# One pool of four PSUM banks for scores and transposes in three attentions, and the sink column written behind each score

## The chip, the cores and the metric

The kernel runs on 1 core of one Trainium2 chip. The metric is device time in microseconds (us) of one execution. TensorE is called PE below, VectorE DVE, ScalarE ACT, GpSimd POOL, SyncE SP. PSUM, the memory that PE writes its results to, has eight banks here, b0 to b7, each 128 partitions by 512 float32.

## The reference

Three transformer blocks in a row on 512 tokens of width 1024, all in float32:

```python
def reference(x, ...):
    x = first_block(x, ...)    # pooling mixer + attention of 8 heads, gates, then an MLP
    return second_block(x, ...)

def second_block(x, p, ...):
    h = x
    for i in range(2):
        hn = rms_norm(h, attn_norm[i])
        if i % 2 == 0:
            mix = diff_attention(hn, ...)   # 8 heads, softmax(q1 k1) - lambda * softmax(q2 k2), over all 512 keys
        else:
            mix = windowed_gqa(hn, ...)     # 16 query heads, 4 kv heads, |i-j| <= 128, a sink logit per head
        h = h + mix
        h = h + conv_ffn(rms_norm(h, ffn_norm[i]), ...)
        gate = sigmoid(rms_norm(h, ple_norm[i]) @ ple_w_gate[i])
        h = h + (p[i] @ ple_w_proj[i]) * gate
    return rms_norm(h, final_norm)
```

In the sliding attention the sink enters the softmax as one more column: `m = max(max(s), sink)`, `pr = exp(s - m) / (sum(exp(s - m)) + exp(sink - m))`. With sequence 512 the first attention is causal with a slope per head (both key blocks of 256 are attended to where they lie in the past).

## The kernel before, in words

Every matrix product is done in three passes of float32r on split operands (high times high, high times low, low times high). So each step of a linear layer is three matmuls of 128x512 (lines 393, 394, 395), and splitting the weights is work for ACT (line 283) and POOL (line 239).

Python builds one table of steps, and each engine's program runs through that table from top to bottom and issues what is its own. Every engine works in the order of the table and blocks at the first wait that is not yet met. The table's order comes from a small planner at build time. `Schedule` keeps a clock for PE, DVE, ACT and POOL, and `duration` gives each step a planned length. `Flow.run` holds a list of waiting processes, each with a function that returns the events it needs. A step on DVE, ACT or POOL is placed when its events are planned to be ready at PE's clock plus `AHEAD` (0.4 us). A PE step of an attention (scores, transposes, products with V) is placed when its events are `MARGIN` (0.2 us) old on PE's clock. Where none is ripe, the next step of the linear layers is placed. So the linear layers of later heads, and the output projection where it can begin, fill PE between the steps of an attention.

An attention works in blocks of 128 queries, four per head. The chain of one block is:

- `scores`: the score matmuls (lines 407, 408, 409), kind "score". They contract over 64 rows, so two of them run side by side, one on rows 0 to 63 and one on rows 64 to 127 of the array: two heads in `attention_pairs`, the two softmaxes of one head in `attention_diff`. Such a pair takes two banks, b2 and b3 (`sbk`), and `need` asks that both are free.
- `soft`: in the first and third attention DVE adds the mask and takes the row minimum of the negated score in one custom instruction (kind "mask_min", line 599, followed by a short read of its accumulator). That frees the score bank. ACT then takes the exponential (line 328), DVE the reciprocal (line 578), and DVE (line 603) or POOL (line 264) normalizes. In the second attention DVE takes row maxima (line 574), ACT two exponentials (line 323, which free the banks), DVE reciprocal, ratio and the combination of the two (line 586).
- `turns_of`: PE transposes the block (line 415, kind "turn"), into b4 and b5 in turn (`tbk`). ACT (line 334) and DVE (line 621, "turn_low") bring it to SBUF as high and low parts, and the DVE step frees the bank. `v_tile` uses the same two banks for the transposes of V.
- `products_of`: the products with V (lines 438 and 439, in the second attention 426 to 428) into b6 (`obk`).

Linear layers use b0 and b1 (`LB2`) while an attention runs; b7 is for norms.

In the third attention the sink logit must stand in column 384 of the score bank when mask_min reads it; the score itself fills columns up to 384. Head t always has the same bank (b2 for even t, b3 for odd), so `sinks` writes the column once per head: for heads 0 and 1 ahead of all scores, for head t + 2 directly behind the last mask_min of head t (kind "sink_column", line 608, a DVE copy of 128x1). That makes 16 copies.

## Time and profile before

| what | value |
|---|---|
| median of 3 runs | 1973.62 us (1973.46 to 1975.21) |
| profiled execution: first to last instruction | 1972.9 us |
| PE busy | 1940.0 us, 98% |
| DVE busy | 1188.4 us, 60% |
| ACT busy | 924.4 us, 47% |
| POOL busy | 1109.2 us, 56% |
| granted PE clock, mean | 0.997 |

The times of the runs and the span of the profiled execution lie within 0.1% of each other. A PE busy share counts a matmul from its start to a modelled end, and the next one starts before that end, so a stretch can be "busy" although its matmuls start further apart than they could. Start-to-start times of the timeline tell more than the share. The three attentions lie at about 40 to 130 us, 732 to 950 us and 1407 to 1540 us of the span.

### The profile page before, as it was taken

What the parts mean: (1) busy time and instruction counts of PE and PEld (TensorE: products, weight loads), DVE (VectorE), ACT (ScalarE), POOL (GpSimd) and SP (SyncE); (2) the same over time, 40 slices, a digit from 0 to 9 for tenths busy, and PEclk for the clock granted to TensorE, in tenths of its full rate; (3) what the DMA queues carried; (4) which work ended last, traced back from release to release, by engine and by line L of the source; (5) the groups of instructions that cost most, each with busy time, mean ns of one, the idle gap of its engine ahead of it and who ended that gap; (6) DMA issues with size and microseconds to landing.
All of it is one profiled execution on the core that took longest, in us unless ns stands there. A gap on an engine that the chain in (4) does not pass through costs nothing.

```text
span 1972.9 us, 25163 instructions
## 1 busy us (share of the span) xinstructions
PE 1940.0 (98%) x9232; PEld 1590.0 (81%) x9232; DVE 1188.4 (60%) x1952; ACT 924.4 (47%) x1740; POOL 1109.2 (56%) x842
## 2 busy tenths in 40 slices
PE   8999999999999999999999999999999999999997
PEld 6877888888888877777888888888777888888886
DVE  6773325353433488877675646856688675746855
ACT  5653336533333366555453433445477543443443
POOL 5345544454444456454576665755785576666662
PEclk9999999999999999999999999999999999999998
DMA  4122233232232321111322222223110323222321
GB/s 160 65 70 96 89 114 128 95 104 102 97 111 94 111 98 68 45 65 54 128 103 100 97 96 97 97 90 109 65 54 33 128 97 107 97 86 96 107 93 57
DMA packets 52106, 182.72 MB, mean 93 GB/s; under 512 B 5776, under 2 KB 6160, under 8 KB 51984
## 3 DMA queue, kind: packets, MB, share of 16 engines
q1 hardware_dynamic: 51984, 181.12, 26.4%
q8 instruction: 74, 1.21, 0.2%
q14 instruction: 48, 0.39, 0.1%
HBM read 174.80 MB, written 6.29 MB: 92 GB/s over the span
## 4 chain that ended last, share of the span: by engine, by line
PE 92%; DVE 5%; ACT 1%; issue 1%; DMA 0%; POOL 0%; SPq 0%; DVEq 0%; ACTq 0%; POOLq 0%
PE b L393 28%; PE b L395 28%; PE b L394 28%; PE b L415 2%; PE b L407 1%; PE b L448 1%; PE b L439 1%; PE b L438 1%; DVE sm L574 1%; PE b L408 1%; PE b L409 1%; DVE ra L621 1%; DVE fa L586 0%; PE b L426 0%; DVE ra L483 0%
## 5 line engine op out<-in xcount | busy, mean ns | idle before, releaser
L239 POOL TENSOR_TENSOR ra<-raw,ra 128x512 fp32r<-128x512 f32 x632 | 883.2, 1405 | 771.7 <-ACT ra L283 770.0
L393 PE MATMUL b<-ra 128*128 128x512 f32 x2528 | 1000.7, 396 | 15.9 <-POOL ra L239 9.4
L395 PE MATMUL b<-ra 128*128 128x512 f32 x2528 | 985.9, 390 | 0.0
L394 PE MATMUL b<-ra 128*128 128x512 f32 x2528 | 985.2, 390 | 0.0
L283 ACT ACTIVATE ra<-raw 128x512 fp32r<-128x512 f32 x632 | 392.8, 628 | 531.9 <-PE b L395 526.4
L393 PEld LDWEIGHTS b<-ra 128*128 128x128 f32 x2528 | 475.5, 188 | 121.2 <-issue 15.2
L395 PEld LDWEIGHTS b<-ra 128*128 128x128 f32 x2528 | 475.0, 188 | 101.0
L394 PEld LDWEIGHTS b<-ra 128*128 128x128 f32 x2528 | 475.7, 188 | 93.3
L737 DVE TENSOR_TENSOR h<-b,h 128x512 f32<-128x512 f32 x136 | 91.8, 683 | 61.4 <-PE b L395 60.6
L628 DVE TENSOR_TENSOR tmp<-b,rb 128x512 f32<-128x512 f32 x62 | 42.4, 689 | 100.2 <-PE b L395 100.0
L621 DVE TENSOR_TENSOR ra<-b,ra 128x512 fp32r<-128x512 f32 (+4 forms) x166 | 91.9, 567 | 17.6 <-ACT ra L334 14.8
L628 DVE TENSOR_TENSOR gbuf<-b,rb 128x512 f32<-128x512 f32 x54 | 37.1, 690 | 107.7 <-PE b L395 107.5
L334 ACT ACTIVATE ra<-b 128x512 fp32r<-128x512 f32 (+3 forms) x142 | 67.9, 485 | 70.7 <-PE b L415 69.2
L707 DVE TENSOR_TENSOR fa<-b,fa 128x512 f32<-128x512 f32 x56 | 38.6, 689 | 78.8 <-PE b L395 78.8
L291 ACT ACTIVATE ra<-tmp 128x512 fp32r<-128x512 f32 x79 | 49.0, 626 | 56.4 <-DVE tmp L756 19.2
L415 PE MATMUL b<-ident,fa 128*128 128x128 f32 x368 | 63.2, 281 | 3.0 <-DVE ra L621 1.6
L328 ACT ACTIVATE fa<-fa,sm 128x257 f32<-128x257 f32 (+5 forms) x96 | 53.4, 558 | 23.3 <-DVE sm L599 23.0
L483 DVE TENSOR_TENSOR ra<-tmp,ra 128x512 fp32r<-128x512 f32 x60 | 59.4, 1007 | 2.9 <-ACT ra L291 2.4
L415 PEld LDWEIGHTS b<-ident,fa 128*128 128x128 f32 x368 | 41.0, 140 | 21.3 <-issue 9.2
L291 ACT ACTIVATE ra<-gbuf 128x512 fp32r<-128x512 f32 x58 | 36.0, 627 | 43.5 <-DVE gbuf L756 19.9
L489 DVE SCALAR_TENSOR_TENSOR ra<-h,vec,ra 128x512 fp32r<-128x512 f32 x40 | 44.8, 1124 | 9.1 <-ACT ra L296 9.1
L574 DVE TENSOR_REDUCE sm<-b 128x1 f32<-128x512 f32 x64 | 41.0, 681 | 14.9 <-PE b L409 14.7
(276 smaller groups left out, 1900.4 us busy)
## 6 DMA issues: line engine op xcount, KB each, us to landing
raw<-in_f_g SPq DMA_DIRECT2D x40, 512.0 KB, 3.5
raw<-in_f_v SPq DMA_DIRECT2D x40, 512.0 KB, 3.5
raw<-in_f_d SPq DMA_DIRECT2D x40, 512.0 KB, 3.5
raw<-in_w_up SPq DMA_DIRECT2D x32, 512.0 KB, 3.5
raw<-in_w_down SPq DMA_DIRECT2D x32, 512.0 KB, 3.5
raw<-in_p_g SPq DMA_DIRECT2D x16, 512.0 KB, 3.5
raw<-in_w_gp SPq DMA_DIRECT2D x8, 512.0 KB, 3.4
raw<-in_w_ga SPq DMA_DIRECT2D x8, 512.0 KB, 3.4
```

The lines of the kernel that those rows point to most:

```text
L239: e.tensor_tensor(wl, src, wh.bitcast(F), ALU.subtract).then_inc(*w_low.mark(n))
L283: e.activation(wh, src, ACT.Copy).then_inc(*w_high.mark(n))
L291: e.activation(dst, src, ACT.Copy).then_inc(*high.mark(n))
L334: e.activation(dst, src, ACT.Copy).then_inc(*high.mark(n))
L393: e.matmul(ps, wh[:, c:c + 128], xh, start=start, stop=False)
L394: e.matmul(ps, wh[:, c:c + 128], xl, start=False, stop=False)
L395: last = e.matmul(ps, wl[:, c:c + 128], xh, start=False, stop=stop)
L415: x = e.transpose(m.banks[b][:, 128 * q:128 * q + 128], src[:, 128 * q:128 * q + 128], m.ident[:, :])
L574: e.reduce_max(nm, banks[b][:, :], AX, negate=True).then_inc(*soft.mark(n))
L621: e.tensor_tensor(dl, src, dh.bitcast(F), ALU.subtract).then_inc(*low.mark(n))
L628: e.tensor_tensor(z, banks[b][:, :], m.rb[:, :], ALU.mult).then_inc(*evac.mark(n))
L737: e.tensor_tensor(dst, src, hk, ALU.add).then_inc(*evac.mark(n))
```

## The change

Banks b2, b3, b4 and b5 become one pool (`QB`) for scores and transposes alike, in all three attentions and in `v_tile`. `pick` takes the bank that is free earliest on the planner's clock; `picked(2)` asks for two free ones ahead of a pair of scores. Since the bank of a head is no longer fixed, the sink column can't be written once per head: it is written in `soft` for each score, behind the score and ahead of its mask_min. The planned length of the first score of a pair gets 0.35 us on top of its matmuls (0.2 before), the second 0.02 us (0.04 before). The inner loop over `(i2,)` runs once, so scores are still placed one block at a time.

```diff
@@ duration
-            return (3 * (0.012 + a[1] / 2400.0) + 0.2) if a[4] == 0 else 0.04
+            return (3 * (0.012 + a[1] / 2400.0) + (0.35 if a[10] else 0.0)) if a[4] == 0 else 0.02
@@ build
-    sbk = [2, 3]
-    tbk = [4, 5]
+    QB = [2, 3, 4, 5]
     obk = 6
+
+    def picked(n):
+
+        ready = sorted((b for b in QB if bank_free[b] is not None), key=lambda b: sc.time_of(bank_free[b]))
+        return ready[:n] if len(ready) >= n else None
+
+    def pick(l):
+
+        ready = [b for b in l if bank_free[b] is not None]
+        return min(ready, key=lambda b: sc.time_of(bank_free[b])) if ready else None
@@ turns_of (v_tile is changed alike)
-                b = rot(tbk)
+                b = pick(QB)
@@ attention_pairs, soft
             yield 0, "ve", lambda: (score, *made)
+            if sinks:
+                made += sinks(t, b, score)
             n = row("mask_min", x["p"][:, 0:wide], banks[b][:, c0(i):c0(i) + wide], mk, slope(t), nm, score,
                     (*x["free"], *made))
             v = done("ve", "soft_v", n)
             bank_free[b] = (v,)
-            if i == 3 and sinks and t + 2 < 2 * npairs:
-                sinks(t + 2, b)
@@ scores (attention_diff is changed alike)
-                    if len(PB.free) < 2 or None in (bank_free[sbk[0]], bank_free[sbk[1]]):
+                    if len(PB.free) < 2 or picked(2) is None:
                         return None
...
-                if sinks and p + i == 0:
-                    sinks(0, sbk[0])
-                    sinks(1, sbk[1])
...
-                    b = rot(sbk)
+                        b = pick(QB)
@@ second_block_sliding
-        sunk = {}
-
-        def sinks(t, b):
-            sunk[t] = (done("ve", "soft_v", row("sink_column", b, t, bank_free[b])),)
-            bank_free[b] = sunk[t]
+        def sinks(t, b, score):
+            return (done("ve", "soft_v", row("sink_column", b, t, (score,))),)
```

The rest of the diff is indentation and a list `steps` that holds one entry (two in the attentions by pairs).

**Where instructions move.** First place: PE, the first three score pairs of the first attention. Names in square brackets are the semaphores that an instruction waits for: soft_v is DVE's softmax work, evac, low_v and low_p are evacuations and low parts. Before, linear steps lie between one pair and the next; here the pair of 128 columns, two linear steps, and the pair of 256 columns:

```order
L407 MATMUL b2<-ra 128x128 [waits low_p,evac]
L408 MATMUL b2<-ra 128x128
L409 MATMUL b2<-ra 128x128
L407 MATMUL b3<-ra 128x128 [waits evac]
L408 MATMUL b3<-ra 128x128
L409 MATMUL b3<-ra 128x128
L393 MATMUL b6<-ra 128x512
L394 MATMUL b6<-ra 128x512
L395 MATMUL b6<-ra 128x512
L393 MATMUL b5<-ra 128x512 [waits w_low_p]
```

Now the pair of 128 columns (into b5 and b2), the one of 256 (b3 and b4) and the one of 384 (b5 and b2 again) follow each other with nothing between. From the second half of the 256 pair on:

```order
L407 MATMUL b4<-ra 128x256 [waits low_v]
L408 MATMUL b4<-ra 128x256
L409 MATMUL b4<-ra 128x256
L407 MATMUL b5<-ra 128x384 [waits soft_v]
L408 MATMUL b5<-ra 128x384
L409 MATMUL b5<-ra 128x384
L407 MATMUL b2<-ra 128x384 [waits soft_v]
L408 MATMUL b2<-ra 128x384
L409 MATMUL b2<-ra 128x384
```

The same run of three pairs stands at the third and the fourth pair of heads too. Over the whole program 16 of the 80 score pairs now stand directly behind another (none before): 7 in the first attention, 7 in the second, 2 in the third.

Second place: DVE in the third attention. Before, a head's last block, with the copy for the head two further on behind each mask_min (ISA with mask):

```order
L599 ISA fa,sm<-b2,mask 128x257 [waits turned,score]
L599 ISA sm 128x1
L608 COPY b2<-sm 128x1 [waits soft_v]
L599 ISA fa,sm<-b3,mask 128x257 [waits turned,score]
L599 ISA sm 128x1
L608 COPY b3<-sm 128x1 [waits soft_v]
```

Now every block has its copies, ahead of each mask_min, which waits for the copy (soft_v):

```order
L608 COPY b3<-sm 128x1 [waits score]
L599 ISA fa,sm<-b3,mask 128x385 [waits soft_v,turned]
L599 ISA sm 128x1
L608 COPY b5<-sm 128x1 [waits score]
L599 ISA fa,sm<-b5,mask 128x385 [waits soft_v,turned]
L599 ISA sm 128x1
```

There are 64 copies in place of 16.

Third place: PE, the last pair of heads of the third attention, the last two transposed blocks ahead of the last pair of scores. Before, b4 and b5 back to back:

```order
L415 MATMUL b4<-ident,fa 128x128 [waits low_v]
L415 MATMUL b4<-ident,fa 128x128 x2
L415 MATMUL b5<-ident,fa 128x128 [waits elem_p,low_v]
L415 MATMUL b5<-ident,fa 128x128
L407 MATMUL b2<-ra 128x256 [waits soft_v]
```

Now a linear step stands between them, and the second takes a bank that held a score:

```order
L415 MATMUL b3<-ident,fa 128x128 [waits low_v]
L415 MATMUL b3<-ident,fa 128x128 x2
L393 MATMUL b1<-ra 128x512
L394 MATMUL b1<-ra 128x512
L395 MATMUL b1<-ra 128x512
L415 MATMUL b5<-ident,fa 128x128 [waits elem_p,soft_v]
```

The number of PE's instructions is the same (9144 matmuls), and so are SP's loads and their order.

## Rows read from the trace of the kernel before

**Rows 1.** The page: span, busy time by engine, chain by engine.
```profile
span 1972.9 us, 25163 instructions
...
PE 1940.0 (98%) x9232; PEld 1590.0 (81%) x9232; DVE 1188.4 (60%) x1952; ACT 924.4 (47%) x1740; POOL 1109.2 (56%) x842
...
PE 92%; DVE 5%; ACT 1%; issue 1%; DMA 0%; POOL 0%; SPq 0%; DVEq 0%; ACTq 0%; POOLq 0%
```

**Rows 2.** PE's waits, 732:950: who waited for whom, us, times, longest.
```profile
PE b L415 <- DVE fa L586: 0.9, 2, 0.6
PE b L407 <- DVE ra L483: 0.5, 1, 0.5
```

**Rows 3.** PE's waits, 1390:1545.
```profile
PE b L415 <- DVE ra L621: 1.6, 1, 1.6
PE b L393 <- DVE ra L621: 0.9, 1, 0.9
```

**Rows 4.** Timeline of PE at a score pair: start, us, line, out<-in.
```profile
736.48 0.39 PE L394 MATMUL b<-ra 128*128 128x512 f32 x1
736.71 0.39 PE L395 MATMUL b<-ra 128*128 128x512 f32 x1
737.03 0.50 PE L407 MATMUL b<-ra 64*128 64x512 f32 x2
...
737.93 0.50 PE L393 MATMUL b<-ra 128*128 128x512 f32 x1
738.27 0.40 PE L394 MATMUL b<-ra 128*128 128x512 f32 x1
```

**Rows 5.** Timeline of PE and of DVE, a score pair of 128 columns.
```profile
86.18 0.33 PE L407 MATMUL b<-ra 64*128 64x128 f32 x2
...
86.67 0.50 PE L393 MATMUL b<-ra 128*128 128x512 f32 x1
```

**Rows 6.** Timeline of DVE behind that pair.
```profile
86.29 0.69 DVE L628 TENSOR_TENSOR tmp<-b,rb 128x512 f32<-128x512 f32 x1 [2.40 <-PE b L395]
86.90 0.28 DVE L599 CUSTOM_DVE_ANT_0 fa<-b,mask 128x128 f32<-128x128 f32 x1
...
87.31 0.09 DVE L599 DVE_READ_ACCUMULATOR2_ANT sm<- 128x1 f32 x1
87.75 0.16 DVE L578 RECIPROCAL sm<-sm 128x1 f32<-128x1 f32 x1 [0.35 <-ACT fa L328]
87.95 0.29 DVE L603 TENSOR_SCALAR fa<-fa,sm 128x128 f32<-128x128 f32 x1
```

**Rows 7.** Timeline of PE and of DVE in the second attention, a score pair and its combination.
```profile
774.24 0.50 PE L407 MATMUL b<-ra 64*128 64x512 f32 x2
...
778.09 1.40 DVE L586 SCALAR_TENSOR_TENSOR fa<-gbuf,sm,fa 128x512 f32<-128x512 f32 x1
```

**Rows 8.** Line 608, and DVE's timeline at two of its copies.
```profile
L608 DVE COPY b<-sm x16: 148/162/164, 1405.5 to 1508.5; 128x1 f32<-128x1 f32 x16
...
1478.85 0.41 DVE L599 CUSTOM_DVE_ANT_0 fa<-b,mask 128x257 f32<-128x257 f32 x1
1479.19 0.08 DVE L599 DVE_READ_ACCUMULATOR2_ANT sm<- 128x1 f32 x1
1479.31 0.16 DVE L608 COPY b<-sm 128x1 f32<-128x1 f32 x1
1479.42 0.43 DVE L599 CUSTOM_DVE_ANT_0 fa<-b,mask 128x257 f32<-128x257 f32 x1
```

**Rows 9.** Stretches: us, busy by engine, clock, DMA; and line 599 in 1450:1513.
```profile
1410.00:1450.00 40.00, 40.00 (x247) 31.63 (x243) 28.65 (x105) 29.11 (x77) 37.57 (x43) 1.00 0.15 54
1450.00:1513.00 63.00, 62.64 (x412) 50.53 (x411) 55.99 (x182) 50.60 (x132) 40.55 (x53) 1.00 0.13 45
1513.00:1540.00 27.00, 24.79 (x154) 20.17 (x152) 21.56 (x54) 17.06 (x43) 9.30 (x12) 1.00 0.16 55
...
L599 DVE DVE_READ_ACCUMULATOR2_ANT sm<- 128x1 f32 x34 | 2.8, 81 | 0.0
```

More of the change, by code:

```diff
@@ L401, in tensor_program @@
         elif kind == "score":
-            b, nk, c0, (qh, ql), row, (kh, kl), i, lo, free, ready = a
+            b, nk, c0, (qh, ql), row, (kh, kl), i, lo, free, ready, _ = a
             for t in free + ready:
@@ L1258, in need @@
                 def need():
[L1259 removed]
+                    if (t, i) not in p_done or pick(QB) is None or (t and (t - 1, i // 2) not in used):
                         return None
[L1261 removed]
+                    return (p_done[(t, i)], *bank_free[pick(QB)])
                 yield rank0(t) + per * i, "pe", need
@@ L1336, in scores @@
         def scores(p):
-            for i in range(4):
+            for i2 in range(4):
                 def need():
-                    if len(PB.free) < 2 or None in (bank_free[sbk[0]], bank_free[sbk[1]]):
+                    if len(PB.free) < 2 or picked(2) is None:
                         return None
@@ L1342, in need @@
                         return None
[L1343 to L1361 removed]
+                    return (*[t for b in picked(2) for t in bank_free[b]], *Q(2 * p)[3], *KT(2 * p)[3])
+                yield 8 * p + 2 * i2, "pe", need
+                steps = []
+                for i in (i2,):
+                    lo, hi = span(i)
+                    nk = hi - lo
+                    for t in (2 * p, 2 * p + 1):
+                        k, buf, free = PB.get()
+                        nm, su = (sm[:, 24 + 4 * k + z:25 + 4 * k + z] for z in range(2))
+                        b = pick(QB)
+                        qh, ql, rw, qt = Q(t)
+                        kh, kl, krow, kt_ = KT(t)
+                        assert rw == krow
+                        n = row("score", b, nk, c0(i), (qh, ql), rw, (kh, kl), i, lo, bank_free[b], (*qt, *kt_), i == i2)
+                        bank_free[b] = None
+                        wide = mask_of(t, i)[0].shape[-1]
+                        tile[(t, i)] = dict(k=k, p=buf, free=free, nm=nm, su=su, wide=wide, nb=nk // 128)
+                        steps.append((t, i, b, done("pe", "score", n)))
+                for x in steps:
+                    launch(soft(*x))
             scored.add(p)
@@ L1406, in scores @@
         def scores(t):
-            for i in range(4):
+            for i2 in range(4):
                 def need():
-                    if not PB.free or not T.free or None in (bank_free[sbk[0]], bank_free[sbk[1]]):
+                    if not PB.free or not T.free or picked(2) is None:
                         return None
@@ L1412, in need @@
                         return None
-                    return (*bank_free[sbk[0]], *bank_free[sbk[1]], *Q(t)[3], *KT(t)[3])
-                yield 8 * t + 2 * i, "pe", need
-                lo, hi = span(i)
-                k, a, free = PB.get()
-                ti, pb, tfree = T.get()
-                bs, score = [], []
-                for c in range(2):
-                    b = rot(sbk)
-                    qh, ql, _, qt = Q(t)
-                    kh, kl, _, kt_ = KT(t)
-                    r = row("score", b, hi - lo, 0, (qh, ql), 64 * c, (kh, kl), i, lo, bank_free[b], (*qt, *kt_))
-                    bank_free[b] = None
-                    bs.append(b)
-                    score.append(done("pe", "score", r))
-                tile[(t, i)] = dict(k=k, p=a, free=free, ti=ti, pb=pb, pb_free=tfree,
-                                    su=(sum1(t, i), sm[:, 26 + 4 * k:27 + 4 * k]))
-                launch(soft(t, i, bs, score))
+                    return (*[x for b in picked(2) for x in bank_free[b]], *Q(t)[3], *KT(t)[3])
+                yield 8 * t + 2 * i2, "pe", need
+                steps = []
+                for i in (i2,):
+                    lo, hi = span(i)
+                    k, a, free = PB.get()
+                    ti, pb, tfree = T.get()
+                    bs, score = [], []
+                    for c in range(2):
+                        b = pick(QB)
+                        qh, ql, _, qt = Q(t)
+                        kh, kl, _, kt_ = KT(t)
+                        r = row("score", b, hi - lo, 0, (qh, ql), 64 * c, (kh, kl), i, lo, bank_free[b], (*qt, *kt_),
+                                i == i2)
+                        bank_free[b] = None
+                        bs.append(b)
+                        score.append(done("pe", "score", r))
+                    tile[(t, i)] = dict(k=k, p=a, free=free, ti=ti, pb=pb, pb_free=tfree,
+                                        su=(sum1(t, i), sm[:, 26 + 4 * k:27 + 4 * k]))
+                    steps.append((t, i, bs, score))
+                for x in steps:
+                    launch(soft(*x))
             scored.add(t)
@@ L1448, in process @@
             i, z, v = yield from scaled(x, b, tok, 5)
-            yield 0, "pe", lambda: (v, *bank_free[tbk[0]]) if gate() and bank_free[tbk[0]] is not None else None
-            tb = rot(tbk)
+            yield 0, "pe", lambda: (v, *bank_free[pick(QB)]) if gate() and pick(QB) is not None else None
+            tb = pick(QB)
             t = done("pe", "turned", row("turn", tb, z, 4, bank_free[tb], (v,)))
```

19 lines of the change are left out of this document (1 added, 18 removed).

## The prediction

> **What bounds the kernel now.** I read the page first. PE is busy for 98% of the span and is 92% of the chain that ended last; DVE is 5% of that chain [rows 1]. So the kernel is a queue of matmuls, and a change in the attentions can win or lose two things only: time in which PE waits, and time that it loses where one kind of work follows another. Next I asked for PE's waits in the attentions. The first has none over its 90 us. In the second, PE waited 0.9 us in two places for a combined block (line 586) and 0.5 us for the first key part, which is ready late whatever banks there are [rows 2]. In the third, a transpose waited 1.6 us once for line 621, and linear steps 0.9 us [rows 3]. Line 621 is DVE's step that frees a transpose bank. That single 1.6 us is the one wait in the trace that names a bank of the old split: it is the third place of the order, where two transposed blocks stand back to back and b5's last user isn't copied yet. Everywhere else the linear steps cover what two and two banks cost. About 3 us of waits is all that better overlap can give back there.
>
> Then the timeline of PE around a pair of scores. Plain steps start 0.23 us apart (736.48 to 736.71). The pair starts 0.32 us behind the step ahead of it, the next linear step 0.90 us behind the pair's start, and the one after 0.34 us later [rows 4]. Three passes at 0.23 are 0.69. So a pair that stands alone costs 0.09 to enter, 0.21 inside and at its end, and 0.11 behind it: 0.41 us more than its columns. Of that 0.3 us belongs to the two switches (0.09, half of the 0.21, 0.11).
>
> Last, DVE by stretches of the third attention: 28.7 of 40 us busy, then 56.0 of 63, then 21.6 of 27 [rows 9]. In the middle stretch it has 7.0 us left, which is little for an engine that takes its steps in a fixed order.
>
> **The change, part by part.**
>
> *Switches, -3.0 us.* The order shows 16 pairs directly behind another pair, none before. Each saves at most 0.3 us, together 4.8. No row shows a pair behind a pair: the least is nothing, if the second pair pays the same price. Plain matmuls behind each other pay no switch, and that is the nearest row, but the banks that the second pair waits for can pull its two halves apart, and more pairs than before now lie next to linear steps, where they lay next to transposes. I take -3.0 (from -4.8 to 0).
> The Trainium skill, TensorEngine Tiling (Array Packing), Key Properties, says that a change of tiling mode drains TensorE and that tiles of one mode work independently; by that rule all 16 save in full, -4.8. The rows above show the switch; that its price vanishes between two pairs no run here shows.
>
> *Three bursts in the first attention, +0.8 us.* At heads 0, 4 and 6 the third pair needs the banks of the first. A pair of 128 columns takes 0.49 us from start to next start [rows 5] and the one of 256 up to 0.17 more (three passes of 128 columns more, at 0.23 for 512), less 0.3 for the switch, so the third pair is due about 1.0 us behind the first. Its banks come free with mask_min: the second read of the accumulator ended at 87.40, 1.22 us behind the score's start at 86.18, with DVE busy on line 628 until 86.98 [rows 5, 6]. With DVE free it would be 1.1. So PE waits 0.1 to 0.3 us there, or 0.7 more where a step as long as line 628's is in front. I take 0.25 each, +0.8 (0 to 2.4). Behind the waiting score stand one linear step and the first transposes; these need line 603, which now stands behind two more mask_min in DVE's queue, and PE's wait has already covered that.
>
> *Second attention, -0.5 us.* Two pairs can be in flight, so transposes stand further behind their scores: counted in the order at the prices above, the shortest were 5.4 to 5.9 us of PE work, and most are now 6 to 9. That removes the 0.9 us of [rows 2]. But one block (head 2, block 0) has only 4.6 us, where a score that started at 774.24 had its combination begun at 778.09, with two of 0.7 us behind each other [rows 7]: 4.6 us as well, with no slack. I take -0.5 (-0.9 to +2).
>
> *The bank wait of the third attention, -1.0 us.* The third place of the order has a linear step where 1.6 us were waited for [rows 3]. But what was late was DVE's queue, and the bank now taken waits for mask_min in that same queue. -1.0 (-1.6 to 0).
>
> *48 more copies, +2.4 us.* A copy of one column is 0.16 us of DVE, and an independent step starts 0.11 behind it [rows 8]. A step that waits for a short one on its own engine starts 0.20 behind it (line 578 to line 603, 87.75 to 87.95) [rows 6]. Now mask_min waits for the copy, so a copy is 0.20 us of DVE's queue: 64 times 0.20, less 16 times 0.11, is +11 us over the attention, and the same 0.20 is added to the time that a bank is held. In 1450:1513 there are 34 mask_min [rows 9] and 8 copies: 34 times 0.20 less 8 times 0.11 is 5.9 us against 7.0 idle. In 1410:1450 and 1513:1540 the idle 11.4 and 5.4 us are over twice what is added, so linear steps and slack (a block's transposes stand 5 to 20 us behind its scores) hide it. In the middle stretch I let half of the idle time be of use, 3.5 us, since the rest is DVE waiting for others: 2.4 us come through to PE. The upper bound takes 0.32 us a copy: with a copy between them two mask_min start 0.57 us apart, and the first one's read of its accumulator starts after 0.34, which leaves 0.23, and 0.09 more because the second now waits for the copy [rows 8]. 34 times 0.32 less 0.9 less 3.5 is 6.5, and the last stretch adds some 2, together 8.5. The lower bound is 0: all hidden.
> The Trainium skill, VectorE: DVE Perf Modes, The DRAIN you can't avoid, has DVE's pipe empty behind every step, with or without a semaphore, and advises few steps over few semaphores. By it the wait itself is free and 48 copies cost their 0.16, 7.8 us in all, and the middle stretch hides them. The rows differ: 0.11 behind a copy without a wait, 0.20 behind a short step with one.
>
> *Nothing:* SP's loads and their order are the same. POOL's normalizations move with the blocks; POOL is full only at the start of the third attention (37.6 of 40 us), where blocks stand furthest ahead of their transposes, and has over a third of the middle stretch idle (40.6 of 63) [rows 9].
>
> **Sum.** -3.0 + 0.8 - 0.5 - 1.0 + 2.4 = -1.3 us. The profiled execution spans 1972.9 us, 0.7 under the median of the runs; against the median the changed kernel comes to 1972.3. That is inside 0.2% (3.9 us), which is about what a measurement of this kernel can tell from no change.
>
> **The rivals.**
>
> *All of the overlap, none of the cost.* The switches give 4.8, the waits of the second and third attention go (0.9 and 1.6), bursts and copies are hidden: -7.3, 1966.3 us. For it: the planner counts each copy and places linear steps accordingly, and no other stage changes its order. Against it: DVE at 56.0 of 63 us. Chance 0.25.
>
> *DVE becomes the bound of the third attention.* The place is line 608 ahead of line 599 from the fourth pair of heads on. At 0.32 us a copy the middle stretch needs 10.0 us more where 7.0 are idle and half of them usable, and the last one 2 more, +8.5 in place of +2.4; with that, score banks come free later and the gain of the third bank is lost (+1.0). 1972.3 + 6.1 + 1.0 = 1979.4 us, slower than before. It decides from the point where the added time per stretch passes the idle time. For it: the wait of 1.6 us shows a DVE queue that is already late once. Against it: linear steps stand in all of these pairs. Chance 0.25.
>
> *The plan is too slow.* A pair is now planned at 0.35 + 0.06 us over its columns, which is 0.15 more than before, while a pair in a row of pairs takes less than one alone. PE then comes early to scores and transposes in all three attentions: bursts +2.4, second attention +2, and the rest as above: 1972.3 + 1.6 + 2.5 = 1976.4 us. Chance 0.15; still no change.
>
> **How the numbers follow.** The forecast has 0.35. Faster by over 0.2% (under 1969.7): the first rival, and little of the forecast, 0.27. Slower by over 0.2% (over 1977.6): the second rival and a part of the third, 0.25. Within: 0.48. The range runs from 1966 (the first rival) to 1980 (just past the second), and leaves out some 1 in 10 on each side, for costs that I don't see; the forecast's own range is 1969.5 to 1975.
>
> **What would show it.** In PE's timeline at 40 us three pairs behind each other, the second starting about 0.8 us or less after the first for 128 columns, and the third with an idle time of 0.1 to 0.3 us for line 599. In the second attention no wait for line 586. Copies x64 with mask_min 0.20 us behind each; DVE over 95% busy in the middle of the third attention, and PE's waits there 2 to 3 us in sum. It is wrong if PE's waits in the third attention sum to over 6 us, if pairs in a row start as far apart as pairs that stand alone, or if the linear stages, whose order hardly moves, change by over 1 us.

## The result, and the profile after

In seven runs of each on one chip the changed kernel took 1982.01 us (1980.75 to 1983.14) and the kernel before 1975.14 us (1973.46 to 1975.77). The ratio is 1.0037 [1.0027, 1.0047]: slower by some 7 us. The forecast was 1972.3 us in a range of 1966 to 1980, so the time lies outside the range, and on the side to which I gave 0.25.

The page of the changed kernel, which answers to [rows 1]:

```profile
span 1980.9 us, 25252 instructions
...
PE 1942.0 (98%) x9232; PEld 1590.7 (80%) x9232; DVE 1189.5 (60%) x2000; ACT 922.1 (47%) x1740; POOL 1106.5 (56%) x842
...
PE 88%; DVE 9%; ACT 1%; issue 1%; DMA 0%; DVEq 0%; POOL 0%; SPq 0%; ACTq 0%; POOLq 0%
```

PE is 2 us busier, and the span is 8.0 us longer. DVE's share of the chain that ended last went from 5% to 9%. Its busy time rose by 1 us only, but that hides a load in one place: in the third attention it is busy for 110.7 us where it was for 105.0 (the stretches 1411.60:1544.29 and, before, 1407.53:1536.52), while it fell elsewhere.

**Where the time went, by stages.** Linear steps fill PE in every stage, and the change moves some of them from one stage to another. So I took the start of the first score and of the last product with V of each attention, counted the 128x512 matmuls that had run by then, and took 0.2275 us (the distance of plain steps) for each matmul that a stage now has more or fewer. For the second attention that is: before, 732.78 to 932.13 us with 492 such matmuls; after, 733.61 to 931.42 with 471. 197.81 - 199.35 + 21 x 0.2275 = +3.2 us. For the third: 1407.53 to 1536.52 with 264, after 1411.60 to 1544.29 with 258, 132.69 - 128.99 + 6 x 0.2275 = +5.1. All stages of the profiled executions, against before (a plus is time lost):

| stage | change, us | my terms for it, us |
|---|---|---|
| up to the first score, and first attention | -0.4 + 0.7 = +0.3 | -1.3 + 0.8 |
| linear stages between | +0.5 | 0 |
| second attention | +3.2 | -1.3 - 0.5 |
| third attention, and what follows it | +5.1 - 1.1 = +4.0 | -0.4 - 1.0 + 2.4 |

(The -3.0 for the switches is spread here by the 7, 7 and 2 pairs.) The stretch up to the first score differs by up to 2 us between profiled executions of kernels that don't differ there, so the first line is good to about 2 us. The linear stages and the second attention repeat within 0.2 us wherever two kernels of this study share a stage. The third attention repeats within 0.4 (5.1 in the change; 5.4 in e3, e7 and e12, which have the same order there), and what follows it within 0.6.

PE's waits in the second attention, 725:950, which answer to [rows 2] (who waited for whom, us, times, longest):

```profile
PE b L415 <- DVE fa L586: 3.4, 6, 0.7
PE b L415 <- DVE sm L578: 1.5, 2, 0.9
PE b L415 <- DVE ra L621: 1.1, 2, 0.7
PE b L407 <- DVE ra L483: 0.5, 1, 0.5
PE b L407 <- DVE ra L621: 0.2, 1, 0.2
```

6.7 us in twelve waits, where there were 1.4 in three. Eight of them are transposes waiting for the combined block or for a step on its way (lines 578 and 586): the wait that I said would go has grown.

PE's waits in the third attention, 1390:1550, which answer to [rows 3]:

```profile
PE b L393 <- DVE ra L621: 1.3, 1, 1.3
PE b L393 <- DVE h L737: 0.9, 1, 0.9
PE b L393 <- DVE tmp L646: 0.7, 1, 0.7
PE b L407 <- DVE sm L599: 0.3, 1, 0.3
PE b L415 <- POOL fa L264: 0.2, 1, 0.2
PE b L438 <- DVE ra L621: 0.2, 1, 0.2
```

The 1.6 us for a transpose bank are gone, as predicted. Linear steps wait longer for DVE instead (line 621: 1.3 where it was 0.9, line 737: 0.9 where it was 0.4). But the list of the kernel before is longer than the two lines of [rows 3]. For the same window, 1390:1545, it has two more:

```profile
PE b L393 <- DVE tmp L646: 0.7, 1, 0.7
PE b L393 <- DVE h L737: 0.4, 1, 0.4
```

So the sum is 3.6 us in both kernels, while the stage lost 5.1. Most of the loss is in gaps too short to be named. By PE's start-to-start times the gaps between one pass of scores and the next hold 14.96 us (before 13.07, with two gaps fewer), and the 161 between products with V 19.29 (18.18). The view of waits alone would have missed the loss.

Stretches of the third attention after, which answer to [rows 9] (busy time of PE, PEld, DVE, ACT, POOL; clock, DMA):

```profile
1410.00:1450.00 40.00, 40.00 (x250) 31.22 (x249) 30.72 (x126) 29.43 (x80) 36.26 (x43) 1.00 0.18 56
1450.00:1513.00 63.00, 61.63 (x379) 47.15 (x378) 53.93 (x183) 45.77 (x120) 40.64 (x50) 1.00 0.15 50
1513.00:1540.00 27.00, 25.17 (x159) 20.24 (x159) 22.76 (x77) 18.19 (x49) 12.02 (x17) 1.00 0.11 36
```

In the middle PE issues 379 matmuls where it issued 412, at a clock of 1.00 as before.

Now the single steps. PE in the second attention, a pair directly behind a pair (start, us, line):

```profile
736.85 0.40 PE L395 MATMUL b<-ra 128*128 128x512 f32 x1
737.18 0.51 PE L407 MATMUL b<-ra 64*128 64x512 f32 x2
...
737.98 0.40 PE L407 MATMUL b<-ra 64*128 64x512 f32 x2
...
738.78 0.50 PE L393 MATMUL b<-ra 128*128 128x512 f32 x1
739.11 0.39 PE L394 MATMUL b<-ra 128*128 128x512 f32 x1
```

The first pair enters 0.10 late, the two together take 1.60 us for six passes (1.38 at 0.23), and the step behind them is 0.10 late: 0.42 us over the columns for two pairs, where one alone costs 0.41 [rows 4]. The second pair is free. The Trainium skill, TensorEngine Tiling (Array Packing), Key Properties, says that a change of tiling mode drains TensorE. Between two pairs the mode stays, and the rows agree: no price shows there. So 16 pairs were worth up to 6.4 us, more than the 4.8 that I took as the most.

PE in the first attention, the third pair of a burst:

```profile
41.62 0.65 PE L407 MATMUL b<-ra 64*128 64x384 f32 x2 [0.64 <-DVE sm L599]
41.90 0.33 PE L408 MATMUL b<-ra 64*128 64x384 f32 x1
42.07 0.34 PE L409 MATMUL b<-ra 64*128 64x384 f32 x1
42.11 0.33 PE L408 MATMUL b<-ra 64*128 64x384 f32 x1
42.29 0.33 PE L409 MATMUL b<-ra 64*128 64x384 f32 x1
```

It waits 0.64 us for the bank, and then its halves run apart (x1 in place of x2), since one bank came free ahead of the other.

DVE in the third attention, two blocks with their copies, which answers to [rows 8]:

```profile
1499.06 0.15 DVE L608 COPY b<-sm 128x1 f32<-128x1 f32 x1
1499.35 0.43 DVE L599 CUSTOM_DVE_ANT_0 fa<-b,mask 128x257 f32<-128x257 f32 x1
1499.70 0.08 DVE L599 DVE_READ_ACCUMULATOR2_ANT sm<- 128x1 f32 x1
1499.70 0.16 DVE L608 COPY b<-sm 128x1 f32<-128x1 f32 x1
1500.00 0.43 DVE L599 CUSTOM_DVE_ANT_0 fa<-b,mask 128x257 f32<-128x257 f32 x1
```

mask_min starts 0.30 us behind the copy that it waits for, not 0.20 (0.30 is also the median of all 64, which lie between 0.18 and 0.34). Two mask_min are 0.65 apart. 64 copies take 19.2 us of DVE's queue, of which 0.16 each counts as busy, so the busy time shows only half of them.

DVE and then PE in the second attention, around one of the new waits:

```profile
886.21 2.47 DVE L574 TENSOR_REDUCE sm<-b 128x1 f32<-128x512 f32 x4
888.60 0.15 DVE L578 RECIPROCAL sm<-sm 128x1 f32<-128x1 f32 x1
888.79 0.27 DVE L582 TENSOR_SCALAR sm<-sm 128x1 f32<-128x1 f32 x1
889.10 1.69 DVE L586 SCALAR_TENSOR_TENSOR fa<-gbuf,sm,fa 128x512 f32<-128x512 f32 x1
```

```profile
890.94 0.63 PE L415 MATMUL b<-ident,fa 128*128 128x128 f32 x4 [0.58 <-DVE fa L586]
```

Two pairs of scores were in flight, so four row maxima, 2.47 us, stand together in DVE's queue, and the combination of an earlier block stands behind them. PE waits for that combination. Over the 32 blocks of this attention the time from the start of a block's scores to the end of its combination went from 5.9 to 7.3 us in the mean, from 7.7 to 9.8 at most. In DVE's order a later pair's row maxima stand ahead of a combination in 10 of the 32 blocks (in none before). The ten take 6.9 us in the mean and the other 22 even 7.4, so the example is only one form of it: a block also gets late because its own row maxima, and all that follows, stand behind the steps of a pair that is late already.

### The profile page after: what moved, and what is told of

It reads as the page before. It is cut to its first block, busy times and chain, and to the rows that moved or that the text cites. A ratio compares the mean times of both kernels' runs of the same rounds, so it can differ in the third digit from the quotient of the medians.

```text
span 1980.9 us, 25252 instructions
## 1 busy us (share of the span) xinstructions
PE 1942.0 (98%) x9232; PEld 1590.7 (80%) x9232; DVE 1189.5 (60%) x2000; ACT 922.1 (47%) x1740; POOL 1106.5 (56%) x842
## 4 chain that ended last, share of the span: by engine, by line
PE 88%; DVE 9%; ACT 1%; issue 1%; DMA 0%; DVEq 0%; POOL 0%; SPq 0%; ACTq 0%; POOLq 0%
PE b L393 28%; PE b L395 27%; PE b L394 27%; PE b L415 2%; DVE ra L621 1%; DVE sm L574 1%; DVE fa L586 1%; PE b L448 1%; DVE fa L599 1%; PE b L407 1%; PE b L439 1%; PE b L438 1%; DVE h L737 0%; DVE b L612 0%; PE b L458 0%
## 5 line engine op out<-in xcount | busy, mean ns | idle before, releaser
L415 PEld LDWEIGHTS b<-ident,fa 128*128 128x128 f32 x368 | 41.4, 141 | 23.6 <-issue 7.2
L599 DVE CUSTOM_DVE_ANT_0 fa<-b,mask 128x257 f32<-128x257 f32 (+5 forms) x96 | 45.6, 490 | 15.9 <-PE b L409 7.4
L489 DVE SCALAR_TENSOR_TENSOR ra<-h,vec,ra 128x512 fp32r<-128x512 f32 x40 | 44.5, 1116 | 8.8 <-ACT ra L296 8.7
```

The lines of the kernel that those rows point to most:

```text
L415: x = e.transpose(m.banks[b][:, 128 * q:128 * q + 128], src[:, 128 * q:128 * q + 128], m.ident[:, :])
L599: e.tensor_tensor_reduce(p, src, mk, -sl, BIG, ALU.add, ALU.min, nm).then_inc(*soft.mark(n))
```

## The theories

**T1, the second pair in flight.** The pool costs the second attention time because a second pair's row maxima get ahead of combinations in DVE's fixed order. Rival: it is the sharing of banks itself (a transpose held by a score's bank), or the plan, which places transposes too early.

**T2, the copies.** The third attention loses because each copy is 0.30 us in DVE's queue. Rival: it is the pool there, or the order that the planner makes.

**T3, the planned length.** My third rival had the 0.35 us for a score pair as a loss. The other reading: 0.35 + 0.06 is what a lone pair costs [rows 4], so the plan got truer, and the rest of the change is dearer than it looks.

## The experiments

The kernels come in the order in which they ran. What the text gives for a stage is worked out as above, against before.

**The clock in the slowest of them.** In the change and in the kernel before, PE's granted clock is 1.00, the higher of its two levels (2.4 GHz), from 15 us to the last 14 us of the span. Four kernels here fell to the lower one, 0.50 (1.2 GHz), inside the third attention: e1 for 13.7 us in three stretches, e5 for 23.9 in five, e6 for 10.2 in two, e14 for 6.8 in one. Outside of it e1 has three stretches of 3.4 us at 0.50 (at 44.5, 140.1 and 846.7 us), e14 three at about the same places, and e11 one at 45.8 us. The two of e6 (busy time of PE, PEld, DVE, ACT, POOL; clock, DMA):

```profile
1495.98:1499.40 3.42, 3.13 (x12) 2.84 (x13) 1.06 (x4) 0.25 (x2) 0.59 (x2) 0.50 0.02 5
1526.70:1533.53 6.83, 6.68 (x30) 5.85 (x29) 5.08 (x17) 3.69 (x11) 2.43 (x5) 0.50 0.00 0
```

In e6 PE waited in four places, 2.8 us in sum, between 1490.6 and 1496.3 us; the clock fell at the end of the last wait. At this level plain steps start 0.43 us apart (1548.04 to 1548.47 in e1), not 0.23. So a stretch at 0.50 costs up to 0.47 of its length, an estimate from these two distances: at most 6.4 us in the third attention of e1, 11.2 in that of e5, 4.8 in e6, 3.2 in e14. These kernels' losses are therefore waits and, on top, the clock that fell behind them.

**e1_cost_back**: the change with the old planned length.

```diff
-            return (3 * (0.012 + a[1] / 2400.0) + (0.35 if a[10] else 0.0)) if a[4] == 0 else 0.02
+            return (3 * (0.012 + a[1] / 2400.0) + 0.2) if a[4] == 0 else 0.04
```

> Pool of four and the copies as in the change, but a score pair is planned at 0.2 and 0.04 us over its columns, as before. Theory 'plan' (a pair planned 0.15 us too long lets PE come early to the transposes): PE's waits in the second attention fall from 6.7 us to under 3 us and the time to about 1977. Theory 'queue' (two pairs in flight put row maxima ahead of combinations on DVE, whatever a pair is planned at): waits there stay at 5 to 7 us, time 1980 to 1982.

2006.34 us, 1.016 [1.0143, 1.0177]. That is 24 us slower than the change, which neither theory had expected. The second attention lost 7.3 us, the third 20.6. Up to 11 of the 24 are the clock. PE's waits, 1390:1560:

```profile
PE b L438 <- DVE ra L621: 6.3, 4, 2.8
PE b L393 <- DVE ra L621: 3.4, 2, 2.2
PE b L415 <- DVE sm L599: 1.8, 2, 1.1
```

Under the pool the new length is not a cost; without it the change would be much slower.

**e2_cost_only**: the kernel before, with the new planned length and nothing else.

```diff
-            return (3 * (0.012 + a[1] / 2400.0) + 0.2) if a[4] == 0 else 0.04
+            return (3 * (0.012 + a[1] / 2400.0) + 0.35) if a[4] == 0 else 0.02
```

> The kernel before with the planned length of a pair alone changed to 0.35 and 0.02 us; two and two banks, 16 copies. 'Plan': over 3 us slower than before, with 3 to 5 us more of PE's waits in the second attention. 'Queue': within 1.5 us of before, and no new wait.

1971.92 us, 0.9987 [0.9977, 0.9996]: faster than before by 2.6 us, a gain that again neither theory had expected. In the profile -2.6 are in the second attention and -0.9 in the third with what follows it. Against this kernel the change is slower by 10 us, and that is what pool and copies cost together.

**e3_split_diff**: the change with two and two banks in the second attention only.

```diff
+    SB, TB = list(QB), list(QB)
+    def banks_for(split):
+        SB[:], TB[:] = ([2, 3], [4, 5]) if split else (QB, QB)
...
-                b = pick(QB)
+                b = pick(TB)
...
-                        b = pick(QB)
+                        b = pick(SB)
@@ second_block_diff
+        banks_for(True)
```

> The change, but with score banks b2, b3 and transpose banks b4, b5 apart in the second attention alone. 'Queue': 3 to 5 us faster than the change, PE's waits in the second attention back at 1 to 2 us. 'Plan': those waits stay above 4 us. The third attention keeps its loss of some 4 us in both.

1975.01 us, 1.0002 [0.9993, 1.0011]. The second attention is at -2.7, as in e2, where the pool has +3.2. The pool costs it 5.9 us. Both T1 and its rival of shared banks fit.

**e4_no_copies**: the change with the instructions of every engine in the same order, but without the 64 copies. The sinks are then missing from the third attention's softmax.

```diff
         elif kind == "sink_column":
-            e.tensor_copy(banks[b][:, 384:385], m.sink8[:, t:t + 1]).then_inc(*soft.mark(n))
+            pass
...
-            if sinks:
-                made += sinks(t, b, score)
+            keep = dict(sc.last)
+            sunk = sinks(t, b, score) if sinks else ()
+            sc.last.update(keep)
...
+            sc.begun[n] = max(sc.begun[n], sc.time_of(sunk))
```

> The change with every engine's order kept and the 64 copies of the sink column left out (so the sinks do not enter the softmax of the third attention). Theory 'copies' (DVE's added 11 us make the third attention late): the third attention gets 3 to 5 us shorter than in the change, and PE's waits for lines 621 and 737 there fall below 1.5 us. Rival 'order' (the new places of transposes and scores are late by themselves): under 1 us.

1975.03 us, 1.0001 [0.9991, 1.001]. The third attention is at -1.35 in place of +5.07: at the same order the 64 copies cost 6.4 us. Here the gaps between the passes of scores hold 13.09 us, as before the change, while those between products with V stay at 19.07. The second attention is unmoved (+3.2).

**e5_copies_only**: the kernel before (split banks, old planned length), with a copy behind each score. It was built from the changed kernel; shown is how it differs from the one before.

```diff
+            if sinks:
+                made += sinks(t, b, score)
             n = row("mask_min", x["p"][:, 0:wide], banks[b][:, c0(i):c0(i) + wide], mk, slope(t), nm, score,
...
-            if i == 3 and sinks and t + 2 < 2 * npairs:
-                sinks(t + 2, b)
```

> The kernel before (two and two banks, a pair planned at 0.2 and 0.04) with nothing but the copy behind each score, 64 in place of 16. Theory 'copies': the third attention alone loses, 4 us or more against before, since DVE gets 64 times 0.30 less 16 times 0.11, 17 us, more in its queue. Rival 'copies with the pool' (they hurt only where a score and a transpose share banks): under 2 us.

1995.2 us, 1.0106 [1.0091, 1.0121]. The third attention alone lost 23.6 us; no other stage moved. PE's waits, 1390:1560:

```profile
PE b L415 <- DVE ra L621: 9.0, 5, 2.4
PE b L438 <- DVE ra L621: 2.0, 3, 1.4
PE b L393 <- DVE h L737: 1.8, 4, 0.9
```

So the same number of copies costs 6.4 us in one order and 23.6 in another, of which up to 11.2 are the clock. The price of a copy is a fact of DVE; what comes through to PE is a fact of the order around it.

**e6_copy_planned**: the change, with the copy planned nearer its measured length.

```diff
+    if kind == "sink_column":
+        return 0.26
```

> The change, with the copy planned at 0.26 us (0.32 with the hop to mask_min; 0.16 and 0.22 in the change), near the 0.30 us that the trace shows from copy to mask_min. If the loss of the third attention is a plan that knows too little of DVE's queue, it falls by over 2 us (PE gets linear steps in front of late transposes). If DVE has no time left there, it stays within 1 us.

1988.75 us, 1.0074 [1.0057, 1.0091], a miss: the third attention went to +10.6 from +5.1. Of these 5.5 us up to 4.8 are the clock, which fell to 0.50 twice here and never in the change. So a truer length for the copy gave an order with four waits close together, and the fallen clock may have made most of the loss. Why the order came out so stays open.

**e7_late_turns**: the change, with combined blocks of the second attention planned 1.4 us later, so that transposes come later.

```diff
             T.release(x["ti"], v)
+            sc.ended[(v[0].name, v[1])] += 1.4
```

> The change, and in the second attention the combined block is planned ready 1.4 us later, which is by how much the mean time from score to combined block grew from before to the change (5.86 to 7.25 us). 'Queue': PE's waits for line 586 fall below 1.5 us and the second attention gets 3 us shorter or more. If instead the pool itself costs DVE or ACT time there, waits move to other lines and it gains under 1.5 us.

1981.63 us, 1.0038 [1.0025, 1.0051]. PE's waits, 725:960:

```profile
PE b L426 <- DVE ra L621: 3.6, 4, 1.8
PE b L415 <- DVE ra L621: 1.5, 1, 1.5
PE b L393 <- DVE h L737: 1.2, 2, 0.8
```

No wait for line 586 is left, and the stage is at +2.9 all the same: the products with V wait for the low parts instead. Placing the waiter later doesn't help, since the chain itself is late. That speaks against the theory of a plan that is early only for the transposes. The total did not move.

**e8_first_only**: the pool in the first attention only, 16 copies, the new planned length.

```diff
@@ first_block
+        banks_for(False)
@@ second_block_diff, second_block_sliding
+        banks_for(True)
@@ soft
-            if sinks:
-                made += sinks(t, b, score)
+            if i == 3 and sinks and t + 2 < 2 * npairs:
+                sinks(t + 2, b)
...
```

> The pool of four in the first attention alone; second and third with two and two banks, 16 copies; a pair planned at 0.35 and 0.02 us everywhere. If pool and copies make the loss and the planned length is a gain, this is 2 to 5 us faster than before (second attention -2.6 us, third about -1). If the planned length gains nothing by itself, within 1 us of before.

1970.53 us, 0.9984 [0.9975, 0.9993]: 3.1 us faster than before, most of it what e2 has without a pool (-2.7 in the second attention).

**e12_one_pair**: the change with the pool in place, where in the plan a pair of scores of the second attention waits for the exponentials of the pair before. Only one pair is in flight then.

```diff
+            drained[4 * t + i] = e
...
-                    if not PB.free or not T.free or picked(2) is None:
+                    if not PB.free or not T.free or picked(2) is None or 4 * t + i2 - 1 not in drained:
...
-                    return (*[x for b in picked(2) for x in bank_free[b]], *Q(t)[3], *KT(t)[3])
+                    return (*[x for b in picked(2) for x in bank_free[b]], *Q(t)[3], *KT(t)[3], drained[4 * t + i2 - 1])
```

> The change with its pool of four, but in the second attention a pair of scores is placed only when the planner has the two exponentials of the pair before it done, so one pair is in flight at a time. 'Two pairs in flight' (row maxima of the next pair go ahead of the combination in DVE's queue) says: the mean from score to combined block falls from 7.25 us to under 6.1, the second attention goes from 3.2 us longer than before to over 2 us shorter, total about 1975. If sharing banks between scores and transposes is what costs, it stays above +1 us.

1975.9 us, 1.0005 [0.9996, 1.0015]. The second attention is at -2.7, the mean from scores to combination at 5.8 us. PE's waits, 725:960:

```profile
PE b L393 <- DVE h L737: 0.8, 1, 0.8
PE b L415 <- DVE fa L586: 0.7, 2, 0.5
PE b L407 <- DVE ra L483: 0.4, 1, 0.4
```

With four shared banks and one pair in flight all 5.9 us are back. In this attention all four engines have their instructions in the same order as in e3, so only the numbers of the banks differ from it, and the sharing costs nothing. This settles the main part of T1: it is the second pair, not the sharing. That the delay comes by DVE's queue is read from the timelines and from the mean; no run kept two pairs in flight and moved the row maxima.

**e10_split_all**: split banks everywhere, with the 64 copies and the new planned length.

```diff
+        banks_for(True)
```

> The change with two and two banks in all three attentions: 64 copies, a pair planned at 0.35 and 0.02 us. The copies alone (planned at 0.2) cost the third attention 24 us, the whole change 5. If the planned length makes the difference, the third attention is at +3 to +8 us here too, total 1974 to 1979. If the pool does, it stays over +15 us, total above 1985.

1983.57 us, 1.0042 [1.0027, 1.0056]. In the profile the third attention is at +7.5, and +7.7 with what follows it, against +4.0 with the pool. So the pool gains 3.7 us there, beside 64 copies on DVE. The profiled execution is the fastest of the four (1980.21 us, mean clock 0.997); the other three took 1983.21 to 1984.14 us at 0.994 to 0.995, so part of the median is the clock. Against e2, which has the same banks and planned length and 16 copies (third attention +0.45), the copies cost 7.1 us.

**e11_cost_50**: e8_first_only with 0.5 us where 0.35 stood.

```diff
-            return (3 * (0.012 + a[1] / 2400.0) + (0.35 if a[10] else 0.0)) if a[4] == 0 else 0.02
+            return (3 * (0.012 + a[1] / 2400.0) + (0.5 if a[10] else 0.0)) if a[4] == 0 else 0.02
```

> Pool in the first attention alone, 16 copies, a pair planned at 0.5 us over its columns in place of 0.35. A pair that stands alone costs 0.41 us over its columns by the trace, and 0.35 plus the least step of 0.06 is just that. If what helps is a plan that is right, 0.5 is no better, or worse by 1 us or more. If a longer plan simply buys slack, it is faster again by 1 us or more.

1978.5 us, 1.0017 [1.0008, 1.0026], slower than e8 by 6.5 us (the ratios) to 8 (the medians): the first attention +3.9 (up to 1.6 of it the clock), the second +1.6 in place of -2.7. So longer is not better in general; of 0.2, 0.35 and 0.5 the one nearest to the measured 0.41 for a lone pair wins (with the 0.04 of the three passes and the 0.02 of the second score, 0.35 makes 0.41 over the columns).

**e9_act_copies**: the change with the copies on ACT.

```diff
+        elif kind == "sink_column":
+            e.activation(m.banks[b][:, 384:385], m.sink8[:, t:t + 1], ACT.Copy).then_inc(*soft.mark(n))
...
-    if kind in ("reciprocal", "sum_ratio", "sink_column", "eps_sums"):
+    if kind in ("reciprocal", "sum_ratio", "eps_sums"):
         return 0.16
+    if kind == "sink_column":
+        return 0.22
...
+            if sinks:
+                yield 0, "ac", lambda: (score,)
+                made += sinks(t, b, score)
...
-            return (done("ve", "soft_v", row("sink_column", b, t, (score,))),)
+            return (done("ac", "soft_a", row("sink_column", b, t, (score,))),)
```

> The change with the 64 copies of the sink column written by ACT in place of DVE, behind the score and ahead of mask_min. If DVE's queue is what the copies load, the third attention gets at least 3 us shorter than in the change (as it does without copies, 6.4 us). If the hop through one more engine costs as much, or ACT becomes late for the transposed blocks, it is no shorter or longer.

1975.1 us, 1.0006 [0.9996, 1.0015]. The third attention is at -1.0, as good as with no copies (-1.35). Of PE's waits in 1390:1600 one is left, 0.7 us. Here the order changed too, since the copy has another engine and another planned length; e4 has the order of the change. Both together carry T2: it is DVE's queue.

**e13_both**: e12_one_pair and e9_act_copies together, nothing else.

> Both causes mended at once, the pool of four kept: in the second attention one pair in flight, in the third the copies on ACT. If the causes are separate and add, the stages read as in the two runs alone: second attention 2.7 us shorter than before, third with the end some 2 us shorter, total 3 to 6 us under before (1969 to 1971). If they were two sides of one thing, less than 1.5 us under before.

1968.87 us, 0.9974 [0.9965, 0.9984]. In the profile the second attention is at -2.7 and the third with what follows at -2.6; the whole span is 5.9 us under before. It beats both kernels, the change by about 12 us (the two ratios), and e2 by about 2.5. The middle and the last stretch of the third attention:

```profile
1450.00:1513.00 63.00, 62.77 (x414) 49.44 (x413) 55.02 (x176) 53.06 (x168) 39.03 (x52) 1.00 0.11 35
1513.00:1540.00 27.00, 27.00 (x150) 22.45 (x149) 22.07 (x47) 17.10 (x42) 11.15 (x12) 1.00 0.17 59
```

PE is back at 414 matmuls in the middle and has no wait at the end. ACT still has 9.9 us idle there, with 64 more instructions in the program than the change; it had the room that DVE lacked.

**e14_no_copies_02**: e4_no_copies with the old planned length; the sinks are missing from the softmax here too.

```diff
-            return (3 * (0.012 + a[1] / 2400.0) + (0.35 if a[10] else 0.0)) if a[4] == 0 else 0.02
+            return (3 * (0.012 + a[1] / 2400.0) + 0.2) if a[4] == 0 else 0.04
```

> The change without its 64 copies (so the sinks do not enter the softmax) and with a pair planned at 0.2 and 0.04 us. With copies that planned length cost the third attention 15 us more (20.6 in place of 5.1). If the short plan hurts because DVE's queue, filled with copies, stands in wait of scores that come late, the third attention is within 4 us of before here. If the short plan hurts by itself, it is over 10 us longer. The second attention, where nothing changes, is at about +7 us in both.

1996.19 us, 1.0111 [1.0093, 1.013]. Against e4 the short plan costs 12.1 us in the third attention without any copy (+10.7 against -1.35), and 15.5 with the copies (e1 against the change). Less the clock (at most 3.2 and, in e1, 6.4) that is some 9 us both times. So most of what the short plan costs there has nothing to do with copies.

## Why the prediction was wrong

In the runs the change is +6.9 us where the forecast had -1.3. In the profiled executions it is +8.0, so 9.3 above the terms: 5.0 of that in the second attention, 3.0 in the third with what follows it, 1.3 in the rest.

**Switches, -3.0: right in kind, and too small.** A second pair is free; 0.40 is saved for each, not 0.3 at most. Yet no stage shows the gain by itself. In the second attention the same bunching that saves 7 x 0.40 = 2.8 us costs more behind it (8.7 us by these numbers, since 5.9 are lost in sum), and I had costed the two as if one could be had without the other.

**Three bursts, +0.8: not contradicted.** One wait of 0.64 us stands in the row above; the first attention as a whole is within its 2 us of uncertainty, so the size of the term is not shown.

**Second attention, -0.5 (-0.9 to +2): this is the step that failed first.** It was +3.2 for the stage, or 5.9 us worse than the same planned length gives with split banks. I counted how much PE work stands between a block's scores and its transposes, found it longer (6 to 9 us, from 5.4 to 5.9), and took the time from scores to combination for a constant, read from one block [rows 7]. Even that reading was too short: the 1.40 us at 778.09 are one combination (line 586 has one instruction for each of the 32 blocks), not two of 0.7, so that block took 5.25 us against my 4.6 us of PE work. And the time is no constant: two pairs in flight put two more row maxima, about 1.2 us, ahead of some combinations, and the mean rose by 1.4 us, 0.7 of it ahead of a block's own row maxima. In a fixed order every engine's queue has to be counted, not only the waiting one's. e12 and e3 show that the second pair in flight costs the 5.9 us, e7 shows that later placing doesn't mend it.

**Bank wait of the third attention, -1.0: right, and larger beside the copies.** That wait is gone. With 64 copies on DVE the pool gains 3.7 us there (e10 against the change). With the copies on ACT the stage and what follows it are at -2.1 (e9), where split banks with 16 copies have -0.9 (e2): 1.2 us, close to the term. [rows 3] left out 1.1 us of waits for lines 646 and 737, which changes nothing in it.

**48 more copies, +2.4 (0 to 8.5): mis-sized.** All 64 cost 6.4 us at equal order (e4), 6.1 by the move to ACT (e9). The step that failed is the choice of 0.20 us from a reciprocal ahead of a tensor_scalar, where the copy ahead of the custom instruction takes 0.30; my upper bound of 0.32, read from line 608's own rows, was the nearer row [rows 8]. The 34 blocks of the middle stretch at 0.30, less 0.9 for the old copies and 3.5 for usable idle time, come to 5.8 us by my own working, and the last stretch adds to it. By the rule of the Trainium skill, VectorE: DVE Perf Modes, The DRAIN you can't avoid, that a semaphore between two steps costs nothing extra, the copy would cost its 0.16; the rows, 0.30, speak against it for steps as short as this one. The second rival, "DVE becomes the bound of the third attention", is close to what happened in that stage. It had no loss in the second attention, so that its total, 1979.4 us, lies near the measured one is in part luck. The sign that I named for the middle stretch, DVE over 95% busy, was wrong: DVE shows 53.9 of 63 us, since the 0.14 us between a copy's end and its mask_min (1499.21 to 1499.35) is idle in the records.

**"All of the overlap, none of the cost", 1966.3:** neither cost was hidden. With both taken away, one pair in flight and the copies on ACT, e13 spans 5.9 us less than before, 1.4 short of that rival's 7.3.

**"The plan is too slow", a rival for +4 us: wrong in sign.** The longer planned length alone gains 2.6 us (e2), and the change without it would be 24 us slower still (e1), up to 11 of them by the clock. I had the number in hand, 0.41 us for a lone pair in [rows 4] and 0.35 + 0.06 in the plan, and called it too much for PE. How a plan 0.13 us shorter per pair (my 0.15 was not exact) costs some 9 us, and 12 with the clock, in an attention of 32 pairs (4.2 us by simple count) is argued, not shown: PE falls behind the plan, scores come later than DVE's order assumes, and DVE stands at line 608 for them with other work behind. Its waits, 1407:1560 of e1 (engine, tile, line waited for):

```profile
DVE ra L621 <- ACT ra L334: 10.5, 9, 2.3
DVE gbuf L642 <- PE b L395: 5.3, 2, 3.0
DVE b L608 <- PE b L409: 4.6, 6, 2.6
```

The change has 3.3, 3.0 and 2.6 us in those three places in its 1407:1540, so DVE stands more for ACT and for PE; what starts that chain the rows don't say.

**Still open:** why the planner's order with a truer length for the copy (e6) has PE wait four times close together; and whether the saving of adjacent pairs can be had in the second attention with the row maxima placed behind the combination, which I didn't try.

## What to carry to other kernels

Where engines work through a fixed order, more buffers change what stands ahead of what: before you cost deeper overlap as a gain, count the in-order queue of the engine that serves both the new work and the old chain. A planned length should be the measured price of the step where it stands: 0.13 us for each pair were worth 2.6 us alone and 24 with the pool, so try it alone before any change of structure. When a variant is much slower, look at the granted clock before you put all of it down to waits. A tiny instruction with a dependent one behind it costs the time from start to start (0.30 us here), not its busy time (0.16), and belongs on an engine with idle time in that stretch.

## What was unexpected in the hardware

A copy of 128x1 on DVE holds back the custom instruction that waits for it by 0.30 us from start to start, although it is busy for 0.16; a reciprocal holds back a tensor_scalar by 0.20. A second pair of half-array scores directly behind a first costs almost nothing over its columns (0.42 us for two, 0.41 for one), but where it waits for two banks that come free at different times its halves run one behind the other (41.62 to 42.29 us). The combination of line 586, one and the same operation of 128x512, took from 0.75 to 1.86 us in the changed kernel, with the median at 0.93; the planner counts one length for it. In four kernels with more waits of PE (e1, e5, e6, e14) the granted clock fell from 1.00 to 0.50 for 3.4 or 6.8 us at a time, and plain steps were then 0.43 us apart, not 0.23.
